# Decode attention with all of its key and value transfers asked for by the sync engine, an early key ring and two PSUM banks in turn

## The reference

```python
s_c = einsum(q, k_cmp) + bias;  p_c = softmax(s_c);  o_c = p_c @ v_cmp        # 64 compressed blocks
imp = sum of p_c over heads, two blocks to one; top 16 of the blocks are selected
s_s = einsum(q, selected keys) + bias;  p_s = softmax(s_s);  o_s = p_s @ selected values
s_w = einsum(q, window keys) + bias;  p_w = softmax(s_w);  o_w = p_w @ window values
mix = g0 * o_c + g1 * o_s + g2 * o_w
```

## Time and profile before

| | before |
|---|---|
| median of 3 runs | 1083.4 us (1083.2 to 1086.03) |
| the profiled execution, its own time | 1077.82 us |
| its span, first to last instruction | 1075.8 us |
| mean granted TensorE clock | 0.894 |
| TensorE busy (matmuls) | 909.5 us, 85% |
| VectorE, ScalarE, GpSimd busy | 520.5, 374.1, 99.6 us |
| DMA | 112.43 MB, 105 GB/s mean |

### The profile page before, as it was taken

One profiled execution on the slowest core, in us unless ns is written; L12 is line 12 of the kernel. 1 busy time (PEld: TensorE's weight loads), 2 busy tenths in 40 slices (PEclk: granted clock), 3 DMA queues, 4 the chain that ended last, 5 costly groups with the idle time before them and its releaser, 6 DMA issues.

```text
span 1075.8 us, 19843 instructions
## 1 busy us (share of the span) xinstructions
PE 909.5 (85%) x7903; PEld 813.8 (76%) x7903; DVE 520.5 (48%) x1100; ACT 374.1 (35%) x742; POOL 99.6 (9%) x164
## 2 busy tenths in 40 slices
PE   5804999998977876788887986999999999999994
PEld 5704888776866655455557975999999999999992
DVE  3600234652332456656674246666767676422325
ACT  5201235464521101045573126434344434222214
POOL 1000222334035100200000000000000000000000
PEclk9956999999989755558899998999999999999996
DMA  7344778777435100140003210223222222222212
GB/s 262 80 59 98 233 258 284 252 210 227 143 104 189 57 6 1 40 169 1 2 1 112 73 57 20 99 79 97 80 93 85 83 95 72 89 83 86 87 32 84
DMA packets 53134, 112.43 MB, mean 105 GB/s; under 512 B 6945, under 2 KB 30274, under 8 KB 52594
## 3 DMA queue, kind: packets, MB, share of 16 engines
q1 hardware_dynamic: 45648, 91.68, 27.3%
q0 software_dynamic: 6528, 17.83, 5.4%
q10 hardware_dynamic: 866, 1.65, 0.5%
HBM read 102.92 MB, written 12.38 MB: 107 GB/s over the span
## 4 chain that ended last, share of the span: by engine, by line
PE 73%; DVE 9%; ACT 6%; issue 5%; another core or an unknown queue 4%; DMA 2%; POOLq 1%; POOL 0%; ACTq 0%; SPq 0%; DVEq 0%
PE q L1624 27%; PE q L1622 25%; PE q L2061 2%; PE q L2079 2%; PE q L2089 2%; PE q L1949 1%; PE q L1673 1%; DMA arena<-in_pool 1%; PE q L2003 1%; PE q L2122 1%; PE q L1661 1%; PE q L2123 1%; ACT xt L955 1%; DVE xt L1486 1%
## 5 line engine op out<-in xcount | busy, mean ns | idle before, releaser
L458 DVE TENSOR_TENSOR wring_r<-wring,whi_r 128x1024 fp32r<-128x1024 f32 (+1 forms) x101 | 120.5, 1194 | 394.2 <-ACT whi_r L455 393.9
L455 ACT ACTIVATE whi_r<-wring 128x1024 fp32r<-128x1024 f32 (+1 forms) x101 | 104.3, 1034 | 317.2 <-PE q L1624 313.9
L1624 PE MATMUL q<-xt_r,whi_r 128*128 128x288 f32 x552 | 165.5, 300 | 0.0
L1622 PE MATMUL q<-xt_r,whi_r 128*128 128x256 f32 x552 | 156.5, 283 | 0.0
L1622 PE MATMUL q<-arena_r,whi_r 128*128 128x256 f32 x440 | 135.9, 309 | 20.0 <-DVE xt_r L458 11.9
L1624 PE MATMUL q<-arena_r,whi_r 128*128 128x288 f32 x440 | 132.4, 301 | 0.0
L1624 PE MATMUL q<-arena_r,wring_r 128*128 128x288 f32 x440 | 131.9, 300 | 0.0
L1622 PE MATMUL q<-arena_r,wring_r 128*128 128x256 f32 x440 | 124.8, 284 | 0.0
L1622 PE MATMUL q<-mixt_r,whi_r 128*128 128x256 f32 x400 | 113.0, 282 | 10.6 <-DVE xt_r L458 10.5
L1624 PE MATMUL q<-mixt_r,whi_r 128*128 128x288 f32 x400 | 119.2, 298 | 0.0
L1622 PEld LDWEIGHTS q<-xt_r,whi_r 128*128 128x128 f32 x552 | 106.0, 192 | 0.0
(11 more groups left out here) (403 smaller groups left out, 1620.4 us busy)
## 6 DMA issues: line engine op xcount, KB each, us to landing
wring<-in_w_up SPq DMA_DIRECT2D x42, 512.0 KB, 3.4
wring<-in_w_in SPq DMA_DIRECT2D x27, 512.0 KB, 5.0
arena<-in_pool SPq DMA_DIRECT2D x64, 192.0 KB, 3.5
arena<-in_pool POOLq DMA_DIRECT2D x64, 192.0 KB, 4.0
wring<-in_w_down SPq DMA_DIRECT2D x24, 448.0 KB, 3.3
arena<-in_pool SPq DMA_DIRECT2D x64, 64.0 KB, 2.2
arena<-in_pool POOLq DMA_DIRECT2D x64, 64.0 KB, 2.4
wring<-in_w_out SPq DMA_DIRECT2D x8, 512.0 KB, 6.3
```

Source lines behind the costliest of these rows:

```text
L455: return eng.activation(out, src, ACT.Copy)
L458: return eng.tensor_tensor(out, src, hi.bitcast(F32), ALU.subtract)
L1622: pe.matmul(out[:, 0, 0:HALF], w, x[:, 0:HALF], start=(kk == 0 and n == 0), stop=(end and n == 2))
L1624: mm = pe.matmul(out[:, 1, 0:HALF + NS], w, x[:, HALF:NT], start=(kk == 0 and n == 0), stop=(end and n == 2))
```

## The change

It does these things:

- **Asking.** GpSimd's loop over the halves goes. The sync engine calls `stream` twice for each half, with part 0 and part 1. The reads of the page table are the same in number and size, all by the sync engine now.
- **Early ring.** The window keys of group 0 are asked for right after the first four weight tiles, ahead of the loop over n. `relrow` is sent by ScalarE, on its own queue, at n = 4 of its loop, behind the copy of the first window keys.
- **Two banks.** Banks 5 and 6 are used in turn (`TURN`) by the score sets and by all other transposed results.
- **Order on ScalarE and VectorE.** ScalarE does the halves of tile n + 1 between the parts of its work on tile n; VectorE takes the scores one half earlier.
- **Selection.** The mask's addition and the maximum over 2080 columns, two instructions, become four `tensor_tensor_reduce` of 512 columns and two small maxima.
- **Values of group 1.** Chunks 4 to 9 go into the pages' ring (`vkey`), free by then, and are asked for at the tail's first half; chunks 0 to 3 at steps 1 and 2, chunks 10 to 15 at steps 7 to 9.
- **Constants.** ScalarE asks for `cols` first, for seven others behind the first high part, and for `cst` behind the third part of the inputs.

```diff
+TURN = {b: n for n, b in enumerate(b for half in decode_halves() for b in score_sets_of(*half) + bundles_of(*half))}
...
+        vkey = arena[:, 8224:11296].rearrange("p (k s c) -> p k s c", k=6, s=SG)
...
+        def values_home(g, c):
+            if g < GROUPS - 1 or c < V_RING:
+                return vring[:, c % V_RING], v_land[c % V_RING], 16 * SG * (PAGES // V_RING * g + c // V_RING + 1), c - V_RING
+            if c < 10:
+                return vkey[:, c - V_RING], pg_land[c - V_RING], 16 * (len(ITEM) // PAGE_RING) + 16 * SG, None
+            if c < 14:
+                return vring[:, c - 10], v_land[c - 10], 16 * SG * (PAGES // V_RING * g + 2), c - 10
+            return vkey[:, c - 14], pg_land[c - 14], 16 * (len(ITEM) // PAGE_RING) + 2 * 16 * SG, c - 10
...
             rows = page_rows(kind, PAGES * SG * g + c, PAGES, SG)
-            eng.wait_ge(v_used, (V_RING + PAGES) * g + c + 1)
+            home, land, _, behind = values_home(g, c)
+            if behind is None:
+                eng.wait_ge(pg_used, SG * PAGES * GROUPS)
+            else:
+                eng.wait_ge(v_used, (V_RING + PAGES) * g + V_RING + behind + 1)
...
-                if 7 <= i < 13:
+                if g < GROUPS and 7 <= i < 13:
                     stream_values(eng, kind, g - 1, 2 * i - 10 + part)
+                if g == GROUPS and i == -SG:
+                    for c in range(V_RING + part, 10, 2):
+                        stream_values(eng, kind, g - 1, c)
+                if g == GROUPS and 7 <= i < 10:
+                    stream_values(eng, kind, g - 1, 2 * i - 4 + part)
...
-            issued = [0]
+            issued = [[0], [0]]
+            for i in range(-SG, 0):
+                for part in range(2):
+                    stream_keys(sp, mybir.EngineType.SP, part, 0, i)
+                    issued[part][0] += 1
+            sp.wait_ge(consts, NCONST)
             for n in range(ZT):
-                if n == 4:
-                    sp.wait_ge(rel_sb, 1)
-                    sp.wait_ge(consts, NCONST)
-                    sp.dma_start(relrow.ap(), ohp[0:8, NREL:2 * NREL].unsqueeze(1).broadcast_to([8, 128, NREL])) \
-                        .then_inc(rel_out, 16)
-                    for i in range(-SG, 0):
-                        stream_keys(sp, mybir.EngineType.SP, 0, 0, i)
-                        issued[0] += 1
                 for _, (g, i, h) in HALVES[n]:
-                    stream(sp, mybir.EngineType.SP, 0, issued, g, i, h)
+                    for part in range(2):
+                        stream(sp, mybir.EngineType.SP, part, issued[part], g, i, h)
...
-            issued = [0]
-            for n in range(ZT):
-                if n == 4:
-                    pool.wait_ge(consts, NCONST)
-                    for i in range(-SG, 0):
-                        stream_keys(pool, mybir.EngineType.Pool, 1, 0, i)
-                        issued[0] += 1
-                for _, (g, i, h) in HALVES[n]:
-                    stream(pool, mybir.EngineType.Pool, 1, issued, g, i, h)
...
+            constant(col, "cols")
             split_hi(act, 0)
+            for dst, name in ((c32, "c32"), (relp, "relp"), (ohp, "ohp"), (hm, "hm"), (wpad, "wpad"), (ptab, "ptab"),
+                              (sm[0:32, 0:8], "m0")):
+                constant(dst, name)
             for k in range(KD):
                 act.wait_ge(xin[k // 2], 16)
                 high(act, arena_hi[:, k, :], xt[:, k, :]).then_inc(x_hi, 1)
+                if k == 2:
+                    constant(cst, "c128")
...
             for n in range(ZT):
-                for _, half in HALVES[n]:
-                    decode_half(*half)
+                steps = HALVES[n + 1] if n + 1 < ZT else []
                 if n + 2 < ZT:
                     split_hi(act, n + 2)
                 else:
                     act.wait_ge(w_used, n + 1)
+                for _, half in steps[0:1]:
+                    decode_half(*half)
...
+                for _, half in steps[1:2]:
+                    decode_half(*half)
...
                 if n == 4:
+                    act.wait_ge(rel_sb, 1)
+                    act.dma_start(relrow.ap(), ohp[0:8, NREL:2 * NREL].unsqueeze(1).broadcast_to([8, 128, NREL])) \
+                        .then_inc(rel_out, 16)
...
+                for _, half in steps[2:]:
+                    decode_half(*half)
...
-                s3 = score[:, p, 0:PAST].rearrange("p (n c) -> p n c", n=NBLK)
                 dve.wait_ge(nd_se, QUADS * (p + 1))
-                link(dve.tensor_tensor(s3, s3, bc(left, PAST // NBLK), ALU.add))
-                negated_max(8, score[:, p, :]).then_inc(ns_x, 1)
+                for u in range(QUADS):
+                    s3 = score[:, p, 512 * u:512 * u + 512].rearrange("p (n c) -> p n c", n=8)
+                    dve.tensor_tensor_reduce(out=s3, in0=s3, in1=bc(left[:, 8 * u:8 * u + 8], PAST // NBLK), scale=1.0,
+                                             scalar=-3e38, op0=ALU.add, op1=ALU.max, accum_out=top8[:, u:u + 1])
...
+            def next_bank(*name):
+                n = TURN[name]
+                if n >= 2:
+                    old = in_turn[n - 2]
+                    if old[0] != "scores":
+                        pe.wait_ge(nd_te, BUNDLE[old] + 1)
+                    elif old[2] == 0:
+                        pe.wait_ge(nd_wr, old[1] + 1)
+                    else:
+                        pe.wait_ge(nd_se, QUADS * old[1] + old[2])
+                return bank[5 + n % 2]
```

More of the change, by code:

```diff
@@ L173, in bundles_of, with score_sets_of @@
     return names
+def score_sets_of(g, i, h):
+    if h == 1:
+        return []
+    out = [("scores", g - 1, QUADS)] if i == -SG and 1 <= g <= GROUPS else []
+    return out + ([("scores", g, i // SG)] if g < GROUPS and i >= 0 and i % SG == 0 else [])
+TURN = {b: n for n, b in enumerate(b for half in decode_halves() for b in score_sets_of(*half) + bundles_of(*half))}
 BUNDLE = {b: n for n, b in enumerate(b for half in decode_halves() for b in bundles_of(*half))}
@@ L736, in bundle @@
                 act.wait_ge(nd_t, BUNDLE[name] + 1)
-                return bank[5]
+                return bank[5 + TURN[name] % 2]
             def keys_t(g, i):
@@ L1123, in window_scores @@
                     dve.wait_ge(nd_te, BUNDLE["window", g - 1, True] + 1)
-                dve.tensor_tensor(sw[:, 0:512], bank[6], biasw, ALU.add).then_inc(nd_wr, 1)
+                dve.tensor_tensor(sw[:, 0:512], bank[5 + TURN["scores", g, 0] % 2], biasw, ALU.add).then_inc(nd_wr, 1)
             def window_max(g):
@@ L1143, in past_scores @@
                     dve.wait_ge(rel_out, 16)
-                n = 512 if u < QUADS - 1 else 384
-                ins = dve.tensor_scalar(score[:, g, 512 * u:512 * u + n], bank[6][:, 0:n], biasw[:, 100:101], None,
+                n, t = 512 if u < QUADS - 1 else 384, bank[5 + TURN["scores", g, u + 1] % 2]
+                ins = dve.tensor_scalar(score[:, g, 512 * u:512 * u + n], t[:, 0:n], biasw[:, 100:101], None,
                                         ALU.add)
                 if n < 512:
-                    ins = dve.tensor_tensor(score[:, g, 1920:2048], bank[6][:, n:512], biasw[:, 384:512], ALU.add)
+                    ins = dve.tensor_tensor(score[:, g, 1920:2048], t[:, n:512], biasw[:, 384:512], ALU.add)
                 ins.then_inc(nd_se, 1)
@@ L1205, in decode_half @@
                 if h == 0:
+                    if g < GROUPS and i == 0:
+                        window_scores(g)
+                    if g < GROUPS and i in (4, 8, 12):
+                        past_scores(g, i // 4 - 1)
+                    if 0 <= p < GROUPS and i == -4:
+                        past_scores(p, QUADS - 1)
                     return
                 if g < GROUPS:
-                    if i == 1:
-                        window_scores(g)
-                    if i in (5, 9, 13):
-                        past_scores(g, i // 4 - 1)
                     if i == 6:
@@ L1633, in by_k @@
                 return lambda k: t[:, k, :]
+            in_turn = list(TURN)
+            def next_bank(*name):
[9 more added lines that the diff above has]
+                return bank[5 + n % 2]
             def bundle(*name):
-                if BUNDLE[name] >= 1:
-                    pe.wait_ge(nd_te, BUNDLE[name])
-                return bank[5]
+                return next_bank(*name)
             def copied(*name):
@@ L1679, in scores_d @@
             def scores_d(g, j):
-                n = SETS * g + j
                 copied("keys", g, SG * j - 1)
-                if n >= 1:
-                    before, was = (n - 1) // SETS, (n - 1) % SETS
-                    if was == 0:
-                        pe.wait_ge(nd_wr, before + 1)
-                    else:
-                        pe.wait_ge(nd_se, QUADS * before + was)
+                t = next_bank("scores", g, j)
                 for s in range(SG):
```

(7 more changed lines are left out.)

10 lines of the change are left out of this document (5 added, 5 removed).

## The result

The changed kernel takes **1155.12 us** (median of 4 runs, 1153.86 to 1155.65) against 1083.3 us for the kernel before in the same session: ratio 1.0657, 95% interval 1.0636 to 1.0679. It is 71.8 us slower; the forecast was 51 us slower, and the time lies 5 us above its range. The profiled execution took 1155.47 us with a span of 1153.7 us and a mean clock of 0.863 (before 1077.82, 1075.8 and 0.894), so between the two profiled executions the difference is 77.7 us.

What follows compares the result with a forecast made beforehand. It took TensorE's 43.3 us wait for window keys behind `relrow`, and the sync engine's issuing, as the bound. Terms 0 - 12 + 4 + 49 + 10 = +51 us gave 1129 us profiled, 1134 us as median; range 1095 to 1150.

Steps and rivals of the forecast that it cites:

- start: First high part: weights some 2 us sooner, but ScalarE issues eight transfers first; taken as 0, bounds -2 and +2 us.
- early ring: Up to step 3 of group 0: the 43.3 us wait goes, pages stall beside `relrow` instead; 12 us gained.
- asking, steps 3 to 15 of group 0: Twelve steps where asking takes the sync engine 4.39 us against TensorE's 4.05: +4 us.
- window keys, to step 0 of group 1: Stretch between the groups: the sum has no term for it, 0 us.
- group 1, step 0 to the last page: Sync engine asks for 14 steps of pages and 8 pairs of chunks: 131 us against 82.2, +49 us.
- tail: After group 1: 65.7 us of issuing, 2.2 to land and 8 behind, 76 us against 65.4: +10 us.
- behind the tiles: Everything after the tiles is untouched: 0 us.
- bound of 2: Smallest gain allowed for the early ring, 2 us, if the price adds to `relrow`'s own rows.
- row for row: While `relrow` runs, one page or weight row passes for each of its rows on its 8 engines, 1024 in all.
- Rival A: Early pages: `relrow` passes beside them without holding them, step 3 at about 79, 1102 us; chance 0.21.
- rival C: Early pages: page rows add to `relrow`'s own, so it costs 10 us more, 1144 us; chance 0.11.
- Rival B: Sync engine: asking costs nothing that is not hidden, only the stall counts, 1036 us; chance 0.10.

Runs made afterwards that it cites:

- experiment 8: The changed kernel with `relrow` sent as two transfers of half a row each (1280 B instead of 2560 B): 1154.0 us, ratio 1.0657.
- experiment 1: The changed kernel with GpSimd asking for part 1 again, the early ring and everything else kept: 1067.1 us, ratio 0.9841.
- experiment 2: The kernel before with one edit, the sync engine asking for both parts and GpSimd for none: 1164.69 us, ratio 1.0742.
- experiment 3: The changed kernel with `relrow` in two hops and constant page numbers instead of page-table reads: 1032.05 us, against 1116.87 with the reads.
- Experiment 9: The changed kernel with two askers and `relrow` in two hops (1036.23 us), scores back in their own bank and VectorE's half back in place: 1029.55 us.
- experiment 7: The changed kernel with `relrow` back in the sync engine's queue, ahead of the pages and sooner, early ring kept: 1146.37 us, ratio 1.0568.

## Why the prediction was wrong in size and right in kind

The sum by its own steps, against the profiled execution:

| step | predicted | measured | how it is read |
|---|---|---|---|
| start | 0 | in the early ring's term | first high part at 6.62 instead of 8.81 |
| early ring, to step 3 of group 0 | -12 | -1.6 | 121.13 - 122.73 |
| asking, steps 3 to 15 of group 0 | +4 | +4.4 | 52.3 against 47.9 us |
| window keys, to step 0 of group 1 | 0 | +3.9 | 179.0 to 197.36 against 176.0 to 190.65, and 0.2 ahead of them |
| group 1, step 0 to the last page | +49 | +53.4 | 135.6 against 82.2 us |
| tail | +10 | +15.7 | 81.1 against 65.4 us, from the first scores to the end |
| behind the tiles | 0 | +2 | 736.4 against 734.3 us |
| sum | +51 | +77.8 | |

Some 6 us of the difference vanish in the medians, because the profiled execution before was 5.6 us faster than its median and the one after wasn't.

**The step that failed** is the early ring: "So step 3's last page lands just behind the end of `relrow`, at about 111 us". It landed at 119.4. The term was mis-sized: 1.6 us gained, not 12, 0.4 us beyond the bound of 2 that I had kept, and this is the largest single part of the miss, 10.4 of 26.8 us. By the end of `relrow` 16 pages and three weight tiles were to have passed it, one row for each of its rows; the trace has 7 pages and one weight tile landed by then. Two things went otherwise than in the sum.

First, for some 16 us nothing got through the engines that `relrow` held. From 60 to 74 us only halves of pages passed, 64 rows of each of three, and the page asked for at 59.65 landed at 79.55. From there on the pace was near my row for row: 8.6 to 8.9 rows of `relrow` on each of its engines between one page's 8 rows and the next page's. The Trainium skill says in "DMA: Bandwidth & Descriptors", section "Queues, rings and completion order", that an engine typically drains some 9 to 17 descriptors before it turns to the next queue, and I had priced that rule at 5 us. The 8.6 to 8.9 rows here and the 13 half rows of experiment 8 don't decide between it and my turns, and neither of the two accounts for the first 16 us.

Second, and priced nowhere: the asking engine is slowed while `relrow` runs, to 4.0 to 4.3 us for a read of the table (0.46 otherwise) and 3.6 to 4.6 us for every second request (0.34 otherwise). One engine asked for a pair of pages every 9.5 us, and had asked for 12 of the 16 pages by 109 us. My sum let the asking begin to cost only at step 3. With two engines asking beside the same `relrow` (experiment 1) step 3's last page lands at 114.8, near the forecast. The two things together cost the whole head start but 1.6 us; how they share it stays open, and so does why a store slows the engines that ask. My timing of `relrow` was right in its length: 53.6 us, from 57.5 to 111.1.

**Rival A fell**: `relrow` did hold the pages. So did **rival C** in its mechanism, since `relrow` wasn't lengthened by the page rows, though its +10 is the size of the early ring's miss: that is chance. **Rival B fell**, shown by experiments 1 and 2: asking by one engine costs 80 to 88 us. The rule of the Trainium skill that speaks for it, same page, section "Issuing engines are not separate DMA queues", is that sequencer time is usually small against the DMA itself. That agrees with experiment 3 for the starts alone, which were hidden, and not with starts that have page numbers read first.

**Group 1** was right in kind: 12.6 to 13.7 us from one block of values to the next against 12.3, with no pause in the queue. The missing 4.4 us are single requests that took 0.5 to 1.5 us more than usual, here and there in the queue. I didn't find their cause.

**The window keys** show a cost that I had called hidden: the two-bank turn. A tile that was free of VectorE before now takes the bank that a score held, and TensorE waits 3.33 us for it. Experiment 9 measures the turn and the scores' place together at 6.7 us.

**The tail** is 1.4 us from the first scores to the first read, 67.3 us of asking (65.7 predicted), 2.2 us to the last value products and 10.2 us behind them, where 8 were taken from rows 10. I had carried over the 8 us of a stretch at clock 1.00; here TensorE had been waiting for values, and the granted clock of 395 to 418 us averages 0.70 in this row:

```profile
395.00:418.00 23.00, 15.10 (x112) 12.80 (x110) 2.19 (x6) 0.27 (x1) 0.16 (x1) 0.70 0.24 68
```

**A number that came out right by luck:** without the terms for asking (4 + 49 + 10), my sum gives 1071 us for the change with two askers, and experiment 1 measured 1067.1. The terms don't bear it out. In the profiled execution of experiment 1, whose span is 7.3 us shorter than before, step 3 of group 0 comes 10.9 us sooner, but 5.8 of that are gone by step 15, 3.1 more by step 0 of group 1 and 1.1 in group 1. The tail gains 10.5 us (54.9 against 65.4), where my sum had nothing for the early values and the selection, and 4.1 are lost behind the tiles. With one asker the tail's gain is lost as well; that is the largest part of why the asking costs 88 us and not the 63 of my three terms.

## What to carry to other kernels

Price an engine that only issues transfers like any other: count all that it executes for a transfer, above all the reads that come before it, times the transfers of a step, and compare with the step; here the starts were hidden and the reads cost 85 us. A slow transfer is not made harmless by giving it a queue of its own: of a wait of 43 us that won 1.6 us, and sending `relrow` in two hops won 43. Remove what makes it slow (here a store out of 8 partitions) first, for then the reordering of the keys is worth little. When an edit moves a transfer, compare when it starts before a gain is put down to its queue. When an engine gets late, carry over no duration from a stretch at another clock.

## What was unexpected of the hardware

- While the broadcast store from 8 partitions ran, each read of two numbers of a table in SBUF by the sync engine took 4.0 to 4.3 us (0.46 otherwise) and every second DMA request 3.6 to 4.6 us (0.34 otherwise), with the store on another queue and on the same one (experiment 7). GpSimd's reads were as slow (3.9 to 4.3 us in experiment 1), GpSimd's own requests were not (0.54 to 0.57 us). A faster transfer of the same rows from DRAM, with the DMA engines at 98%, left the reads at 0.47 us.
- The same 1024 rows of 2560 bytes took 53.6 us from 8 partitions of SBUF and 13 us from DRAM, 351 against 108 ns for a row in the mean.
- A page asked for 4 us after that store landed only 19.9 us later, half of its rows at once and the other half after 74 us; the transfers behind it landed 3.7 to 3.9 us apart. With the store's rows cut to 1280 bytes it was 17.2 us, and 2.9 us between the first three.
